# Sixty-two throwaway 64-column products more on TensorE in a network of fp32 matmuls

## The chip, the cores and the metric

The kernel runs on one core of one Trainium2 chip. The metric is the device time of one execution in microseconds (us). The median of three runs of the kernel before is 2643.28 us, from 2640.35 to 2643.76.

## What is computed

A chain of 16 blocks is applied to 256 tokens of width 1024, all in fp32. First come four pairs of a mixer and an MLP. The mixers are a gated delta rule (twice, `gdn`), an mLSTM (`mlstm`) and a differential attention (`diff`). The MLP is `square(relu(h @ w1)) @ w2` with a hidden width of 4096. Then come two layers of four blocks each: a SwiGLU block of width 2816 (`ffn1`), a hybrid mixer of a gated scan and a forgetting attention (`hybrid`), a cross attention on 256 memory tokens (`cross`) and a second SwiGLU block (`ffn2`). Every block ends by adding to the stream:

```python
def sq_relu_mlp(h, w1, w2):
    return jnp.square(jax.nn.relu(h @ w1)) @ w2
...
def swiglu(h, w_gate, w_up, w_down):
    return (jax.nn.silu(h @ w_gate) * (h @ w_up)) @ w_down
...
        h = rms_norm(x, norm_g[i, 2])
        x = x + rms_norm(sq_relu_mlp(h, mlp_w1[i], mlp_w2[i]), norm_g[i, 3])
```

## The kernel before, in words

**Precision.** A product of two fp32 matrices is made of three products of rounded parts. ScalarE rounds a slab of weights to `wH` (line 1517), and VectorE takes the remainder `wL` (line 2167). The activations are split in the same way into `hH` and `hL`, or into areas of the tile `hidden_parts`. TensorE then sums `wH*hH`, `wH*hL` and `wL*hH` into one PSUM region. The helper `three` (line 630) issues this for one 128 x 256 output: eight chunks of the contraction times three pairs, so 24 products. Each product loads a 128 x 128 stationary operand and streams 256 columns. All TensorE products go through the helper `mm`, so the trace shows nearly all of them under line 621, and they are told apart by their tiles.

**Weights.** They come in slabs of 1 MB. A slab of an input projection is 256 output channels wide, so two calls of `three` use it, 48 products. `to_channels` (line 696) makes channels by tokens, with the weights as the stationary operand. `to_tokens` (line 711) makes tokens by channels, with the activations stationary, one call of `three` for each tile of 128 tokens. It is used for the "value" slabs: four in `mlstm`, four in `diff` (there each of the eight tiles is called by itself, between two heads of the attention, by `values`, line 1324), two in each `hybrid`, and four in the second `cross`.

**The order of a part.** A part is one block. `first_products` (line 653) opens each of the 16 parts. It interleaves the products of the part's first two slabs, 96 in all, so that they can follow the activations chunk by chunk: it waits for `low_split` of the first slab (line 660), then for `hH_ready` before each pair of chunks (line 670), later for `hL_ready`. Ahead of it TensorE makes the sum of squares of the norm, and while the norm is finished on the other engines it has other work or nothing. Behind eight of the parts this is `fill` (line 731), 48 products of a memory projection that a later block needs, issued in pieces; elsewhere it is `keep_running` (line 727), plain products of ones.

**The delta rule.** In `gdn` the 16 slabs of the projection are the loop at line 1070. From its fifth slab on it waits until the bank written four slabs ago has been read (`evac`, line 1079). Other steps stand between slabs: score products behind slab 7, and transposes `turn_values` of four blocks behind slabs 11 to 14. Slab 15 stands apart, behind `leaf_level`.

**The throwaway product.** `settle` (line 723) issues one product of 64 columns into a region that the next product overwrites, so its result is used by nothing. It stands in front of the second half of slabs 2 and 9 of `mlp_w1`, in front of the second half of steps 2 and 12 of the SwiGLU projections, and before the fifth slab of each down projection (lines 704, 895, 904, 920, 929), 24 times in all:

```python
            def settle(last, bank, c0):
                mm(ps[:, bank, c0:c0 + 64], hL[:, 1, 0:P], hH[:, 0, 0:64], True, True)
```

Of the kernel before, what the change touches and what calls it, by code (L numbers as in the profile page):

```python
# [15 lines left out]
P = 128  # L16
T = 256
# [146 lines left out]
def program(nc, io, out, parts=None):  # L164
# [30 lines left out]
    with ExitStack() as ctx:  # L195
# [5 lines left out]
        def sem(name):  # L201

            if not name.startswith(SHARED):
                name = scope[0] + name
            if name not in sems:
                sems[name] = ctx.enter_context(nc.semaphore(name))
            return sems[name]
# [39 lines left out]
        onesR = sb("onesR", [P, T], F32R)  # L247
# [368 lines left out]
        def _(pe):  # L616
# [13 lines left out]
            def three(dst, w, x, chunks, before=None, first=True, last=True, second="x"):  # L630


                ins = None
                for pair in (((0, 0), (0, 1), (1, 0)) if second == "x" else ((0, 0), (1, 0), (0, 1))):
                    for k in range(chunks):
                        if before:
                            before(pair, k)
                        ins = mm(dst, w[pair[0]](k), x[pair[1]](k), first and pair == (0, 0) and k == 0,
                                 last and pair == ((1, 0) if second == "x" else (0, 1)) and k == chunks - 1,
                                 **({"skip_group_check": True} if chunks == 1 else {}))  # L640
                return ins
# [11 lines left out]
            def first_products(name, layer, js, c, at, src=(hH, hL), together=True):  # L653


                n = [slab_no[(name, layer, j)] for j in js]
                xH, xL = src
                high_w = [high(n[0], c)] + ([high(n[1], c)] if together else [])
                low_w = [low(n[0], c), low(n[1], c)]
                pe.wait_ge(sem("low_split"), n[0] + 1)  # L660

                def both_halves(b, w, x, k, start=False, ends=False):
                    for m in range(2):
                        ins = mm(ps[:, 4 + b, m * T:(m + 1) * T], at(w, k, m), x[:, k, :],
                                 start and k == 0 and m == 0, ends and k == DC - 1 and m == 1,
                                 skip_group_check=True)
                    return ins

                for k0 in range(0, DC, 2):
                    pe.wait_ge(sem("hH_ready"), W.next("hH_ready"))  # L670
                    for k in (k0, k0 + 1):
                        both_halves(0, high_w[0], xH, k, start=True)
                    for k in (k0, k0 + 1):
                        both_halves(0, low_w[0], xH, k)
                    for k in (k0, k0 + 1) if together else ():
                        both_halves(1, high_w[1], xH, k, start=True)
                if not together:
                    high_w.append(high(n[1], c))
                    for k in range(DC):
                        both_halves(1, high_w[1], xH, k, start=True)  # L680
                for k in range(DC):
                    if k % 2 == 0:
                        pe.wait_ge(sem("hL_ready"), W.next("hL_ready"))
                    last = both_halves(0, high_w[0], xL, k, ends=True)
                last.then_inc(sem("products_done"), 1)
                for k in range(DC):
                    both_halves(1, high_w[1], xL, k)
                pe.wait_ge(sem("low_split"), n[1] + 1)
                for k in range(DC):
                    last = both_halves(1, low_w[1], xH, k, ends=True)  # L690
                last.then_inc(sem("products_done"), 1)
# [4 lines left out]
            def to_channels(name, layer, j, bank, src=(hH, hL), free=None, settled=False):  # L696

                n = slab_no[(name, layer, j)]
                wh, wl = high(n, DC), low(n, DC)
                if free and j >= 4:  # L700
                    pe.wait_ge(sem(free), W.next(free))
                for m in range(2):
                    if settled and m == 1:
                        settle(last, bank, T)
                    last = three(ps[:, bank, m * T:(m + 1) * T],
                                 [lambda k: wh[:, k, m * P:(m + 1) * P], lambda k: wl[:, k, m * P:(m + 1) * P]],
                                 [lambda k: src[0][:, k, :], lambda k: src[1][:, k, :]], DC,
                                 low_weights(n, (1, 0)) if m == 0 else None)
                last.then_inc(sem("products_done"), 1)

            def to_tokens(name, layer, j, bank, src=(hH, hL), tiles=range(TT)):

                n = slab_no[(name, layer, j)]
                wh, wl = high(n, DC), low(n, DC)
                for i in tiles:
                    last = three(ps[:, bank, i * T:(i + 1) * T],
                                 [lambda k: src[0][:, k, i * P:(i + 1) * P], lambda k: src[1][:, k, i * P:(i + 1) * P]],
                                 [lambda k: wh[:, k, :], lambda k: wl[:, k, :]], DC,
                                 low_weights(n, (0, 1)) if i == 0 else None, second="w")
                if TT - 1 in tiles:  # L720
                    last.then_inc(sem("products_done"), 1)

            def settle(last, bank, c0):

                mm(ps[:, bank, c0:c0 + 64], hL[:, 1, 0:P], hH[:, 0, 0:64], True, True)

# [162 lines left out]
            def mlp(i):  # L889
                first_products("mlp_w1", i, (0, 1), DC, columns)  # L890
                summed_norm()
                for j in range(2, 16):
                    if j == 2:
                        filler_out(filled_before[("mlp", i)])
                    to_channels("mlp_w1", i, j, bank_of(j), free="bank_read", settled=j in (2, 9))
                    if i == 0 and j == 3:
                        summed_norm(3, "xsq_summed")

                def floor():
                    pe.wait_ge(sem("bank_read"), W.next("bank_read", 4))  # L900
                    norm_floor()

                down_product("mlp_w2", i, 32, range(0, 32, 2), floor, end_by_pairs=True,
                             at_fifth=lambda last: settle(last, 4, 0))
                post_sum(pair_first=True, on_floor=True, filler=fills[("mlp", i)], upto=34 if i == 2 else 48)

            def ffn(kind, l):
                first_products(kind, l, (0, 1), 2 * DC, lambda w, k, half: w[:, half * DC + k, :], src=ffn_x,
                               together=(kind, l) == ("ffn1", 0))
                summed_norm()  # L910
                for n in range(2, 22):
                    u = slab_no[(kind, l, n)]
                    wh, wl = high(u, 2 * DC), low(u, 2 * DC)
                    if n == 2:
                        filler_out(filled_before[(kind, l)])
                    if n >= 4:
                        pe.wait_ge(sem("bank_read"), W.next("bank_read"))
                    for half in range(2):
                        if n in (2, 12) and half == 1:
                            settle(last, 4 + n % 4, T)  # L920
                        last = three(ps[:, 4 + n % 4, half * T:(half + 1) * T],
                                     [lambda k: wh[:, half * DC + k, :], lambda k: wl[:, half * DC + k, :]],
                                     [lambda k: ffn_x[0][:, k, :], lambda k: ffn_x[1][:, k, :]], DC,
                                     low_weights(u, (1, 0)) if half == 0 else None)
                    last.then_inc(sem("products_done"), 1)

                def settled(last):
                    pe.wait_ge(sem("bank_read"), W.next("bank_read", 4))
                    settle(last, 4, 0)

                down_product(f"{kind}_w_down_2", l, 22, range(22), at_fifth=settled)

# [15 lines left out]
            def gdn(i):  # L948
# [121 lines left out]
                for p in range(2, 16):  # L1070
# [6 lines left out]
                        break  # L1077
                    if p >= 4:
                        pe.wait_ge(sem("evac"), evacuated(p - 4))
                    to_channels("gdn_w_in", j, GDN_ORDER[p], 4 + p % 4)  # L1080
                    if j == 0 and p == 2:
                        pe.wait_ge(sem("vector_setup"), VECTOR_SETUP["params_ready"])
# [1811 lines left out]
```

## Time and profile before

| | us |
|---|---|
| median of three runs | 2643.28 |
| lowest and highest run | 2640.35, 2643.76 |
| profiled execution, its own time | 2639.53 |
| its span, first to last instruction | 2637.8 |
| TensorE busy in it | 2578.1 (98%) |
| VectorE busy | 1668.8 (63%) |
| ScalarE busy | 1357.2 (51%) |
| granted TensorE clock, mean | 0.997 |

The profile holds one execution. Around its span of 2637.8 us lie 1.7 us that the time of 2639.53 also counts. TensorE's matmuls are pipelined, and the end of each is modelled: a row of 8 products that spans 1.07 us does not mean that the next row begins 1.07 us later. The distance from the start of one row to the start of the next is the time that the row's products took, and all working with paces below uses starts.

### The profile page before, as it was taken

To read this page: it belongs to the slowest core of one execution; us is meant where nothing else is said; L and a number is where in the kernel's file an instruction comes from. 1 tells how busy PE (TensorE), PEld (TensorE's weight loads), DVE (VectorE), ACT (ScalarE), POOL (GpSimd) and SP (SyncE) were. 2 spreads that over 40 slices of the span, in tenths; PEclk is the share of its full clock that TensorE was granted. 3 is DMA by queue.
4 is the path that set the end of the run, shared out by engine and by line. 5 is a ranking of instruction groups with operands and counts; after the bars stand their busy time and mean duration, and the time that the engine had idled before them with its cause. 6 is when DMAs were issued, how large, how long until landed. Compare 5 with 4: busy or idle time off the path is not lost.

```text
span 2637.8 us, 48807 instructions
## 1 busy us (share of the span) xinstructions
PE 2578.1 (98%) x21538; PEld 2516.6 (95%) x21538; DVE 1668.8 (63%) x1988; ACT 1357.2 (51%) x1687; POOL 163.0 (6%) x259
## 2 busy tenths in 40 slices
PE   8999999999999999999999999999999999999998
PEld 8989999899998999999999999999999999999998
DVE  5667556575586655676646656756656657764764
ACT  5745445554456544665535445555445436544543
POOL 4400000000020000420000000000000000000000
PEclk9999999999999999999999999999999999999999
DMA  7515565456554664533666765444766755344763
GB/s 215 170 33 160 193 239 164 144 180 224 181 168 148 193 240 148 155 122 118 206 240 171 195 225 169 135 154 136 198 195 185 196 194 161 113 136 138 195 196 128
DMA packets 430995, 452.43 MB, mean 172 GB/s; under 512 B 14114, under 2 KB 395792, under 8 KB 428608
## 3 DMA queue, kind: packets, MB, share of 16 engines
q1 hardware_dynamic: 417952, 416.05, 50.6%
q0 software_dynamic: 8336, 32.87, 3.6%
q8 instruction: 170, 2.79, 0.4%
q10 hardware_dynamic: 4496, 0.39, 0.1%
q14 instruction: 41, 0.34, 0.0%
HBM read 441.15 MB, written 7.60 MB: 170 GB/s over the span
## 4 chain that ended last, share of the span: by engine, by line
PE 85%; DVE 6%; ACT 6%; DMA 1%; issue 1%; POOL 1%; ACTq 0%; SPq 0%; DVEq 0%
PE ps L621 84%; ACT wH L1517 2%; DVE wL L2167 2%; ACT hidden_parts L1577 1%; DMA ring<-in_gdn_w_in 0%; DVE arena L2742 0%; ACT L1544 0%; POOL arena L508 0%; PE ps L1052 0%; DVE hT L2423 0%; POOL arena L510 0%; PE ps L1270 0%; DVE sq L2250 0%; DVE arena L2431 0%; DMA arena<-leaf_out 0%
## 5 line engine op out<-in xcount | busy, mean ns | idle before, releaser
L2167 DVE TENSOR_TENSOR wL<-ring,wH 128x2048 fp32r<-128x2048 f32 x392 | 898.6, 2293 | 744.6 <-ACT wH L1517 744.2
L1517 ACT ACTIVATE wH<-ring 128x2048 fp32r<-128x2048 f32 x392 | 753.6, 1922 | 988.8 <-PE ps L621 986.6
L621 PE MATMUL ps<-hidden_parts,wH 128*128 128x256 f32 x6656 | 989.5, 277 | 3.8 <-ACT hidden_parts L1577 2.8
L621 PEld LDWEIGHTS ps<-hidden_parts,wH 128*128 128x128 f32 x6656 | 899.6, 188 | 5.9 <-issue 3.6
L621 PE MATMUL ps<-hidden_parts,wL 128*128 128x256 f32 x3328 | 693.2, 276 | 1.5 <-DVE wL L2167 1.5
L621 PEld LDWEIGHTS ps<-hidden_parts,wL 128*128 128x128 f32 x3328 | 521.9, 188 | 1.8 <-DVE wL L2167 1.8
L621 PE MATMUL ps<-hH,wH 128*128 128x256 f32 x2624 | 366.1, 281 | 6.4 <-DVE hH L2184 3.1
L621 PE MATMUL ps<-hH,wL 128*128 128x256 f32 x2624 | 358.9, 278 | 3.5 <-DVE wL L2167 3.5
L621 PE MATMUL ps<-hL,wH 128*128 128x256 f32 x2624 | 347.7, 279 | 0.0
L621 PEld LDWEIGHTS ps<-hH,wH 128*128 128x128 f32 x2624 | 329.1, 189 | 12.6 <-issue 10.5
L621 PEld LDWEIGHTS ps<-hH,wL 128*128 128x128 f32 x2624 | 326.9, 188 | 4.3 <-DVE wL L2167 4.3
L621 PEld LDWEIGHTS ps<-hL,wH 128*128 128x128 f32 x2624 | 323.2, 189 | 0.0
L621 PE MATMUL ps<-arena 128*128 128x128 f32 (+1 forms) x1392 | 227.3, 309 | 16.2 <-ACT arena L1941 7.2
L621 PEld LDWEIGHTS ps<-arena 128*128 128x128 f32 x1392 | 193.9, 192 | 34.7 <-ACT arena L1941 9.6
L621 PE MATMUL ps<-sq,onesR 128*128 128x256 f32 (+1 forms) x184 | 64.2, 483 | 4.5 <-ACT sq L1599 2.8
L2423 DVE SCALAR_TENSOR_TENSOR hT<-hT,arena 128x255 f32<-128x255 f32 (+1 forms) x144 | 61.7, 497 | 7.5 <-ACT hT L1751 7.2
L2323 DVE TENSOR_TENSOR arena<-ps,rs 128x512 f32<-128x512 f32 x88 | 60.3, 685 | 0.1
L621 PEld LDWEIGHTS ps<-sq,onesR 128*128 128x128 f32 x184 | 33.5, 197 | 19.8 <-issue 7.3
L621 PE MATMUL ps<-hidden_parts 128*128 128x256 f32 x384 | 51.3, 288 | 0.0
L621 PEld LDWEIGHTS ps<-hidden_parts 128*128 128x128 f32 x384 | 48.1, 191 | 0.6
L2278 DVE TENSOR_TENSOR arena<-arena,ps 128x512 f32<-128x512 f32 x64 | 43.6, 681 | 5.6 <-ACT arena L1669 5.6
L1686 ACT ACTIVATE hidden_parts<-arena 128x512 fp32r<-128x512 f32 x64 | 40.2, 629 | 11.6 <-DVE arena L2278 11.6
(324 smaller groups left out, 1971.7 us busy)
## 6 DMA issues: line engine op xcount, KB each, us to landing
ring<-in_mlp_w SPq DMA_DIRECT2D x128, 1024.0 KB, 5.4
ring<-in_ffn_w_gate SPq DMA_DIRECT2D x88, 512.0 KB, 4.0
ring<-in_ffn_w_up SPq DMA_DIRECT2D x88, 512.0 KB, 5.3
ring<-in_ffn_w_down SPq DMA_DIRECT2D x44, 1024.0 KB, 5.0
ring<-in_gdn_w_in SPq DMA_DIRECT2D x32, 1024.0 KB, 5.9
ring<-in_w_in SPq DMA_DIRECT2D x28, 1024.0 KB, 5.4
hidden_parts<-mem_parts POOLq DMA_DIRECT2D x14, 1024.0 KB, 6.9
ring<-in_mlstm_w_in SPq DMA_DIRECT2D x12, 1024.0 KB, 5.3
```

The lines of the kernel that those rows point to most:

```text
L621: return pe.matmul(o, l, r, start=start, stop=stop, **k)
L1517: f(wH[:, n % PARTS, :], ring[:, n % RING, :], ACT.Copy).then_inc(sem("high_split"), 1)
L1577: ins = f(x_parts[0][:, k, :], xT[:, k, :], ACT.Copy, scale=column(gain, k0 + k))
L1686: f(hidH[:, 2 * g:2 * g + 2, :], two(prod_s[:, g % 2, :]), ACT.Copy).then_inc(sem("hiddenH_ready"), 1)
L2167: tt(wL[:, n % PARTS, :], ring[:, n % RING, :], wH[:, n % PARTS, :].bitcast(F32), ALU.subtract)\
L2278: tt(prod_s[:, g % 2, :], act_s[:, g % 2, :], ps[:, 4 + g % 4, :], ALU.mult)\
L2323: tt(two(act_s[:, n % 2, :]), two(ps[:, 4 + n % 4, :]), rs_twice(), ALU.mult)\
L2423: ins = stt(dst, src, w, dst, ALU.mult, ALU.add)
```

## The change

One throwaway product of 64 columns is added in three kinds of places:

- in `first_products`, behind the wait for the first slab's low part and ahead of the wait for the first activations, into bank 4 from `onesR`: once in each of the 16 parts
- in `to_tokens`, in front of each tile of 128 tokens: 8 times each in `mlstm`, `diff` and the second `cross`, 4 times in each `hybrid`, 32 in all
- in the loop of `gdn`, in front of slabs 8 to 14: 7 times in each of the two, 14 in all

The argument `last` of `settle`, which it did not use, goes. The 24 old ones stay.

```diff
@@ first_products
                 pe.wait_ge(sem("low_split"), n[0] + 1)
+                mm(ps[:, 4, 0:64], onesR[:, 0:P], onesR[:, 0:64], True, True)
...
@@ to_tokens
                 for i in tiles:
+                    settle(bank, i * T)
                     last = three(ps[:, bank, i * T:(i + 1) * T],
...
-            def settle(last, bank, c0):
+            def settle(bank, c0):
...
@@ gdn
                     if p >= 4:
                         pe.wait_ge(sem("evac"), evacuated(p - 4))
+                    if p >= 8:
+                        settle(4 + p % 4, 0)
                     to_channels("gdn_w_in", j, GDN_ORDER[p], 4 + p % 4)
```

The order of TensorE's instructions differs by these additions alone. At the start of the `mlstm` part, behind the 42 fill products (`hidden_parts`), the difference reads:

```order
 L621 MATMUL ps<-sq,onesR 128x256 x3
 L621 MATMUL ps<-hidden_parts 128x256 x42
+L621 MATMUL ps<-onesR 128x64
 L621 MATMUL ps<-hH,wH 128x256 x4
 L621 MATMUL ps<-hH,wL 128x256 x4
```

The new product (+) stands between the fill and the first product of the slab. In the same part, at the value slabs, whose rows have `wH` or `wL` as the moving operand:

```order
 L621 MATMUL ps<-hH,hidden_parts 40x256 x8
+L621 MATMUL ps<-hH,hL 128x64
 L621 MATMUL ps<-wH,hH 128x256 x8
 L621 MATMUL ps<-wH,hL 128x256 x8
 L621 MATMUL ps<-wL,hH 128x256 x8
+L621 MATMUL ps<-hH,hL 128x64
 L621 MATMUL ps<-wH,hH 128x256 x8
```

There one stands in front of every 24 products.

## Rows read from the trace of the kernel before

**Rows 1.** Page: busy time by engine, granted clock, chain that ended last
```profile
PE 2578.1 (98%) x21538; PEld 2516.6 (95%) x21538; DVE 1668.8 (63%) x1988; ACT 1357.2 (51%) x1687; POOL 163.0 (6%) x259
...
PEclk9999999999999999999999999999999999999999
...
PE 85%; DVE 6%; ACT 6%; DMA 1%; issue 1%; POOL 1%; ACTq 0%; SPq 0%; DVEq 0%
```

**Rows 2.** Groups by form: the throwaway products that stand there already
```profile
L621 PE MATMUL ps<-hH,hL 128*128 128x64 f32 x24 | 4.7, 194 | 0.0
```

**Rows 3.** Timeline, PE, 546 to 552: start us, us, engine, line, operation, tiles, count
```profile
546.89 1.10 PE L621 MATMUL ps<-hL,wH 128*128 128x256 f32 x8
547.83 1.12 PE L621 MATMUL ps<-hH,wL 128*128 128x256 f32 x8
548.79 0.20 PE L621 MATMUL ps<-hH,hL 128*128 128x64 f32 x1
548.83 1.17 PE L621 MATMUL ps<-hH,wH 128*128 128x256 f32 x8
549.84 1.07 PE L621 MATMUL ps<-hL,wH 128*128 128x256 f32 x8
550.74 1.07 PE L621 MATMUL ps<-hH,wL 128*128 128x256 f32 x8
```

**Rows 4.** Timeline, PE, 269.9 to 275, another of the 24
```profile
270.84 1.07 PE L621 MATMUL ps<-hH,wL 128*128 128x256 f32 x8
271.75 0.19 PE L621 MATMUL ps<-hH,hL 128*128 128x64 f32 x1
271.78 1.18 PE L621 MATMUL ps<-hH,wH 128*128 128x256 f32 x8
272.80 1.07 PE L621 MATMUL ps<-hL,wH 128*128 128x256 f32 x8
273.70 1.07 PE L621 MATMUL ps<-hH,wL 128*128 128x256 f32 x8
```

**Rows 5.** Timeline, PE, 533 to 538: first products of the second MLP
```profile
532.73 1.84 PE L621 MATMUL ps<-hidden_parts 128*128 128x256 f32 x14
534.40 0.63 PE L621 MATMUL ps<-hH,wH 128*128 128x256 f32 x4
534.88 0.63 PE L621 MATMUL ps<-hH,wL 128*128 128x256 f32 x4
535.35 1.11 PE L621 MATMUL ps<-hH,wH 128*128 128x256 f32 x8
```

**Rows 6.** Timeline, PE: first products behind idle time, two parts, [idle <-releaser]
```profile
217.54 0.71 PE L621 MATMUL ps<-hH,wH 128*128 128x256 f32 x4 [1.33 <-ACT hH L1577]
...
1820.87 0.71 PE L621 MATMUL ps<-hidden_parts,wH 128*128 128x256 f32 x4 [0.59 <-ACT hidden_parts L1577]
```

**Rows 7.** Timeline, PE, value slabs of mlstm: first tile and last tile
```profile
430.00 1.07 PE L621 MATMUL ps<-wH,hH 128*128 128x256 f32 x8
...
449.04 1.07 PE L621 MATMUL ps<-wH,hH 128*128 128x256 f32 x8
```

**Rows 8.** Timeline, PE, value slabs of the second cross: first, second, last tile
```profile
2383.66 2.05 PE L621 MATMUL ps<-wH,hidden_parts 128*128 128x256 f32 x16
...
2386.49 2.05 PE L621 MATMUL ps<-wH,hidden_parts 128*128 128x256 f32 x16
...
2403.45 2.05 PE L621 MATMUL ps<-wH,hidden_parts 128*128 128x256 f32 x16
```

**Rows 9.** Timeline, PE, 766 to 772: first value tile of diff
```profile
768.76 1.10 PE L621 MATMUL ps<-wH,hL 128*128 128x256 f32 x8
769.71 1.10 PE L621 MATMUL ps<-wL,hH 128*128 128x256 f32 x8
```

**Rows 10.** Timeline, PE, second gdn: starts of slabs 9 and 10, inside slab 12
```profile
1112.64 1.11 PE L621 MATMUL ps<-hH,wH 128*128 128x256 f32 x8
...
1118.29 1.11 PE L621 MATMUL ps<-hH,wH 128*128 128x256 f32 x8
...
1130.96 1.07 PE L621 MATMUL ps<-hL,wH 128*128 128x256 f32 x8
1131.87 1.07 PE L621 MATMUL ps<-hH,wL 128*128 128x256 f32 x8
```

**Rows 11.** Timeline, PE, 727 to 730: four narrow products between wide ones
```profile
728.52 0.51 PE L621 MATMUL ps<-onesR,hidden_parts 128*128 128x2 f32 x4
728.89 1.16 PE L621 MATMUL ps<-hH,wH 128*128 128x256 f32 x8
```

More of the change, by code:

```diff
@@ L703, in to_channels @@
                     if settled and m == 1:
-                        settle(last, bank, T)
+                        settle(bank, T)
                     last = three(ps[:, bank, m * T:(m + 1) * T],
@@ L903, in mlp @@
                 down_product("mlp_w2", i, 32, range(0, 32, 2), floor, end_by_pairs=True,
-                             at_fifth=lambda last: settle(last, 4, 0))
+                             at_fifth=lambda last: settle(4, 0))
                 post_sum(pair_first=True, on_floor=True, filler=fills[("mlp", i)], upto=34 if i == 2 else 48)
@@ L919, in ffn @@
                         if n in (2, 12) and half == 1:
-                            settle(last, 4 + n % 4, T)
+                            settle(4 + n % 4, T)
                         last = three(ps[:, 4 + n % 4, half * T:(half + 1) * T],
@@ L928, in settled @@
                     pe.wait_ge(sem("bank_read"), W.next("bank_read", 4))
-                    settle(last, 4, 0)
+                    settle(4, 0)
                 down_product(f"{kind}_w_down_2", l, 22, range(22), at_fifth=settled)
```

## The prediction

> **What bounds the kernel now.** I read the page first: TensorE is busy 98% of the span, its granted clock is at the upper of its two levels, 2.4 GHz, in every slice, and the chain that ended last lies on it for 85% [rows 1]. So nearly every nanosecond of TensorE's own order is a nanosecond of the kernel, and the question is what its products cost each. The groups by form do not tell this, since the ends of products are modelled; I therefore went to the timeline of TensorE and took distances between the starts of rows. What is to be seen there is that the same product, 256 columns with a new stationary operand, runs at two paces. In [rows 7] the value slabs of mlstm take 449.04 - 430.00 = 19.04 us for seven tiles of 24, so 113.3 ns each. In [rows 8] those of cross take 2403.45 - 2383.66 = 19.79 us for as many, 117.8 ns each. I call these the fast and the slow pace. They differ by 4.5 ns, or 4%. No wait is recorded in either stretch, and engines and clock are the same. Once at a pace the stream keeps it until something other than such a product comes between.
>
> The third thing to see is what the 24 throwaway products do that are already there [rows 2]. In [rows 3] one stands behind a slow stretch: the row ahead of it takes 547.83 - 546.89 = 0.94 us for eight products, and the row two behind it 550.74 - 549.84 = 0.90. The stream was slow and is fast. In [rows 4] one stands in a fast stretch: 0.90 or 0.91 before, 0.90 behind. I looked at all 24: 6 of them stand behind a slow stretch and 18 behind a fast one, and behind each of the 24 the pace is fast. That is good evidence that the product does what its name says, where it has wide products before and behind it.
>
> **What one costs.** In [rows 4], from the throwaway product to the second row behind it is 272.80 - 271.75 = 1.05 us, for one throwaway and eight products; eight products alone take 0.91. So one costs 0.14 us, paid in full because the engine has no idle time there. [Rows 3] give the same 1.05 us. The start of the next product lies only 0.03 to 0.04 us behind it, but the product after that comes late, so the 0.03 is not its price. The Trainium skill ("TensorE: Matmul & The Clock Gate", Back-to-back issue gap) gives N/2.4 + 2.5 ns from one isolated warm matmul to the next, 29 ns at 64 columns, and says itself that this leaves out the weight load. At that price my sum below would come out near -5.6 us in place of +0.4; the trace disagrees, with 0.14 us. For a place with narrow products around it the trace has one bound from below: four products of 2 columns take 728.89 - 728.52 = 0.37 us, so 0.09 each [rows 11]. I take 0.14 everywhere, since most places lie between wide products, and keep 0.09 for the range.
>
> One pays for itself if it turns slow into fast for more than 0.14 us / 4.5 ns = 31 products. With this the three kinds of places come apart.
>
> **The first products, 16.** I looked up the stretch in front of each. In eight parts TensorE goes without idle time from fill or from plain products into the slab, and in all eight the first products are slow; [rows 5] are one of them: the rows of the slab follow at 0.47 to 0.48 us for four. There the slow pace lasts for the 96 products of `first_products` in mlstm, diff and both hybrids, where other kinds of products follow, and for 120 in three MLPs and in the first ffn1, until the old throwaway product in slab 2. Saved: 4 x 96 + 4 x 120 = 864 products x 4.5 ns = 3.9 us. Paid: 8 x 0.14 = 1.1. In the other eight parts TensorE is idle for 0.4 to 1.8 us until the first activations have been rounded [rows 6]. The new product waits only for the weights, so it runs in that idle time and costs nothing; for the same reason the stream starts from rest behind it as before, and I count no gain. Of these eight starts four are fast and four slow now, the slow ones for some 30 products each (0.14 us each). This term: 1.1 - 3.9 = -2.8 us.
>
> **The value slabs, 32.** Here one stands in front of every 24 products, less than the 31 that pay for it. In mlstm and the hybrids the stretch is fast already [rows 7]: 16 are paid and nothing is saved. In cross all 192 products are slow [rows 8]: 192 x 4.5 = 0.86 us. In diff each tile stands alone between heads of the attention, and seven of the eight are slow; [rows 9] show one, with 0.95 us for eight. They save 168 x 4.5 = 0.76 us. No idle time of TensorE lies within these stretches that could cover the cost. Paid: 32 x 0.14 = 4.5. This term: 4.5 - 0.86 - 0.76 = +2.9 us.
>
> **The delta-rule slabs, 14.** [Rows 10] show a slow slab, 5.65 us for 48 products, and the inside of a fast one, 0.91 for eight. By the timeline eight of the 14 are slow (slabs 11 and 14 of the first gdn; 8, 9, 10, 11, 13 and 14 of the second) and six fast. Saved: 8 x 48 x 4.5 = 1.7 us. Paid: 14 x 0.14 = 2.0. Slab 15 stands behind other work and keeps its own pace. This term: +0.3 us. Many of these slabs have transposes in front, where no old throwaway product stands, so here it is open whether it works as well.
>
> **The sum.** -2.8 + 2.9 + 0.3 = +0.4 us. Against the profiled execution's own 2639.53 us that gives 2639.9. This execution lies 3.8 us under the median of the runs shown, so against the median it is 2643.7. The 54 products that are paid for cost 7.6 us and win back 7.2: a change that does something at 24 or so places and in which the parts cancel. The weights are not late anywhere for it: ScalarE's rounding waits for TensorE, which frees the slabs, and both other engines are under two thirds busy [rows 1]. Nothing is queued behind a new wait, as there is none.
>
> **Rivals.**
>
> *The throwaway product is cheap.* If its price were the 0.03 us between its start and the next one [rows 3], 54 would cost 1.6 us and the sum would be 1.6 - 7.2 = -5.6 us: 2637.7. The Trainium skill (same page and section) would give 0.03 us as well, by the formula above. For it speaks only that the start of the next product follows so closely; against it stand both readings of 1.05 us. Chance 0.06, with whatever else might make it much faster, such as slow stretches elsewhere falling away as well (all wide products at the slow pace in the span together would be worth about 16 us).
>
> *The pace does not turn where it matters.* The 24 old ones stand within streams of wide products of one kind. The new ones in diff and gdn stand behind narrow products or transposes, those of `first_products` behind fill and with another stationary tile, and a semaphore wait comes between them and the stream. If a stream that begins behind such a change takes its pace anew, all 54 are paid and nothing is saved: +7.6 us, 2650.9, slower by 0.29%. It decides from the point where less than a third of the 7.2 us comes back. For it speaks that streams behind other products and behind idle time start at either pace [rows 6, 10]; against it the 24 of 24. Chance 0.08.
>
> *Luck at the starts.* Each start from rest may fall the other way once times shift by fractions of a microsecond. Eight starts at 0.14 to 0.5 us make about 1 us either way. This is no case by itself but a part of the range.
>
> **How the numbers follow.** A measurement of this kernel tells about 0.2%, 5.3 us, from no change. The forecast, with chance 0.86, lies within that: from 0.09 us as the price of the 22 in narrow surroundings (-1.1), the slow starts from rest turning fast (-0.6) and the runs' own spread below the median (-2.9), which gives 2639.1, up to half of the saving failing (+3.6) and the spread above it (+0.5), which gives 2647.8. I take 2639 to 2648. Faster 0.06, within 0.2% 0.86, slower 0.08.
>
> **What would show it.** In the profile of the changed kernel there must be 24 + 32 + 14 = 70 products of 64 columns with `hL` and 16 with `onesR`. Right: the rows behind fill in the eight parts come at 0.45 us for four and 0.91 for eight; the tile of mlstm's values takes 2.72 + 0.14 = 2.86 us, that of cross goes from 2.83 to the same 2.86; a gdn slab comes at about 5.6 whether it was slow or fast. Wrong: rows at 0.94 behind a new throwaway product (the second rival), or a mlstm tile at 2.75 (the first). The forecast as a whole would be wrong if paces changed in stretches that the change does not touch, above all in the 1,400 products in a row of an MLP, where one change of pace that lasted would be worth up to 6 us.

## The result and the profile after

The kernel got slower. Over 12 runs of each, the median went from 2643.94 us (2637.32 to 2648.22) to 2649.90 us (2647.41 to 2654.55); the ratio is 1.0024, with a 95% interval of 1.0016 to 1.0033. That is +6 us where +0.4 was forecast, above the stated range of 2639 to 2648. The profiled execution took 2647.41 us, with a span of 2645.6 against 2637.8. The clock does not explain the rise: the granted clock averages 0.9952 over the 12 executions of the changed kernel, and 0.9949 to 0.9955 over the executions of before that stand beside the experiments below.

The page of the changed kernel shows what the page of before showed [rows 1], the chain on TensorE for 85% as before, with 62 products more:

```profile
PE 2584.4 (98%) x21600; PEld 2523.9 (95%) x21600; DVE 1669.1 (63%) x1988; ACT 1357.4 (51%) x1687; POOL 161.1 (6%) x259
```

The groups by form of the changed kernel have all 86 products of 64 columns, 70 of the old kind and 16 of ones (compare [rows 2]):

```profile
L621 PE MATMUL ps<-hH,hL 128*128 128x64 f32 x70 | 14.7, 210 | 0.0
...
L621 PE MATMUL ps<-onesR 128*128 128x64 f32 x16 | 3.6, 226 | 2.6 <-DVE wL L2171 2.6
```

So the added products stand where they were meant to. What they do to the pace is in the timeline. First the value slabs of mlstm, which ran at 0.91 us for eight in [rows 7] (start us, us, engine, line, operation, tiles, count):

```profile
433.40 0.19 PE L621 MATMUL ps<-hH,hL 128*128 128x64 f32 x1
...
434.42 1.07 PE L621 MATMUL ps<-wH,hL 128*128 128x256 f32 x8
435.33 1.07 PE L621 MATMUL ps<-wL,hH 128*128 128x256 f32 x8
436.23 0.19 PE L621 MATMUL ps<-hH,hL 128*128 128x64 f32 x1
...
437.29 1.10 PE L621 MATMUL ps<-wH,hL 128*128 128x256 f32 x8
438.23 1.10 PE L621 MATMUL ps<-wL,hH 128*128 128x256 f32 x8
439.18 0.19 PE L621 MATMUL ps<-hH,hL 128*128 128x64 f32 x1
```

The first tile is fast, 435.33 - 434.42 = 0.91 us for eight. The throwaway product at 436.23 has a fast stretch ahead of it and a slow one behind it: 438.23 - 437.29 = 0.94. From throwaway to throwaway the second tile takes 2.95 us, where a tile took 2.72 before. The other six of mlstm's eight tiles read the same, and so do all eight of the two hybrids, which were fast before. In cross, whose tiles were slow before [rows 8], they stay slow, also where the stream ahead is fast, as it is ahead of the first tile:

```profile
2388.91 0.20 PE L621 MATMUL ps<-hH,hL 128*128 128x64 f32 x1
...
2390.91 1.10 PE L621 MATMUL ps<-wL,hidden_parts 128*128 128x256 f32 x8
2391.85 0.19 PE L621 MATMUL ps<-hH,hL 128*128 128x64 f32 x1
```

That is 2391.85 - 2388.91 = 2.94 us a tile where it was 2.83. The first products of mlstm, behind fill, as one of the seven parts of this kind; they answer to [rows 5]:

```profile
404.80 1.72 PE L621 MATMUL ps<-hidden_parts 128*128 128x256 f32 x13
406.36 0.19 PE L621 MATMUL ps<-onesR 128*128 128x64 f32 x1
...
406.94 0.64 PE L621 MATMUL ps<-hH,wL 128*128 128x256 f32 x4
407.41 0.87 PE L621 MATMUL ps<-hH,wH 128*128 128x256 f32 x6
```

The fill itself comes at (406.36 - 404.80) / 13 = 120 ns, and the rows behind it still at 407.41 - 406.94 = 0.47 us for four, the slow pace, in all seven. Last the delta-rule slabs of the second gdn, slow in [rows 10]:

```profile
1111.73 0.28 PE L621 MATMUL ps<-hH,hL 128*128 128x64 f32 x1
...
1112.85 1.07 PE L621 MATMUL ps<-hL,wH 128*128 128x256 f32 x8
1113.76 1.07 PE L621 MATMUL ps<-hH,wL 128*128 128x256 f32 x8
```

Here it works: 0.91 us for eight, and so in 13 of the 14 slabs.

One thing lies beside the change. In this execution part of 24 products of the second cross ran at the lower clock level, behind an idle time of 2.57 us that before has, too (2.56 us). From 2408 to 2424 us the granted clock is 0.89, and 1.00 in the same stretch of before, 2402 to 2418. The 24 products span 7.13 us where they span 5.45 before: 1.7 us of this profile's 7.8. In the profiles of the value tiles alone and of the changed kernel's second set they span 5.45 us again, so it is no part of the cause.

### The profile page after: what moved, and what is told of

Its sections match the earlier page's. It is cut to its first block, busy times and chain, and to the rows that moved or that the text cites. A ratio compares the mean times of both kernels' runs of the same rounds, so it can differ in the third digit from the quotient of the medians.

```text
span 2645.6 us, 48909 instructions
## 1 busy us (share of the span) xinstructions
PE 2584.4 (98%) x21600; PEld 2523.9 (95%) x21600; DVE 1669.1 (63%) x1988; ACT 1357.4 (51%) x1687; POOL 161.1 (6%) x259
## 4 chain that ended last, share of the span: by engine, by line
PE 85%; DVE 6%; ACT 6%; DMA 1%; issue 1%; POOL 1%; ACTq 0%; SPq 0%; DVEq 0%; POOLq 0%
PE ps L621 84%; ACT wH L1521 2%; DVE wL L2171 2%; ACT hidden_parts L1581 1%; DMA ring<-in_gdn_w_in 0%; POOL arena L510 0%; DVE arena L2746 0%; ACT L1548 0%; PE ps L1054 0%; DVE hT L2427 0%; POOL arena L508 0%; PE ps L1274 0%; DVE sq L2254 0%; DVE arena L2435 0%; ACT sq L1790 0%
```

## The experiments

The question was why a product that had turned the pace to fast in 24 of 24 places did not do so in the new ones, and what each of the three groups is worth. The first four runs take the groups apart.

**The first products alone.**

```diff
 in to_tokens and in gdn, against the changed kernel:
-                    settle(bank, i * T)
-                    if p >= 8:
-                        settle(4 + p % 4, 0)
```

> Only the 16 throwaway products of the first products are kept. Theory A (what follows decides the pace; one made of ones behind fill does not turn it): 8 are paid at 0.11 to 0.14 us, nothing is saved, some idle starts move; +1 to +2 us. Rival B (it turns the pace, and the profile of the changed kernel was an odd execution): -2.8 us. In the trace, A has the first products behind fill at 0.94 us for eight, B at 0.91.

Measured: 2645.50 us against 2644.87, ratio 1.0000 (0.9991 to 1.0008). The seven parts behind fill are slow again. The saving of 3.9 us does not exist. The price of the eight that are paid, 1.1 us by the prediction, is too small to be told from nothing here. The expected +1 to +2 us lie inside the interval, at its upper end (+2.1). The eighth part without idle time, the second hybrid, stands behind plain products of ones and not behind fill; it is slow here and fast in the changed kernel.

**The value tiles alone.**

```diff
 against the kernel before, in to_tokens:
+                    settle(bank, i * T)
```

> Only the 32 throwaway products in front of the value tiles are kept. Theory A: each costs 0.11 us or more and leaves the tile slow, 2.94 us from tile to tile where it was 2.72; mlstm and the two hybrids lose 0.2 us a tile, cross 0.1; together +4 to +6 us, less what the slabs behind them gain if those turn fast. Rival B (each costs 0.14 us and the tile is fast, 2.86): +2.9 us.

Measured: 2648.68 us, ratio 1.0017 (1.0009 to 1.0026), so +3.8 us between the medians. Theory A had +4 to +6 less what the slabs behind gain. The timeline has the same pattern as the changed kernel, tile for tile: the throwaway products ahead of mlstm's first three tiles start at 433.31, 436.14 and 439.09, so the first tile takes 2.83 us and the second 2.95.

**The delta-rule slabs alone.**

```diff
 against the kernel before, in gdn:
+                    if p >= 8:
+                        settle(4 + p % 4, 0)
```

> Only the 14 throwaway products of the delta-rule slabs are kept. Theory A (in front of channel slabs it turns the pace, as the 24 old ones do): 0 to +0.5 us, with all slabs but perhaps one at 0.91 us for eight. Rival B (the pace is luck of each execution): some 7 of the 14 slow, +1 us.

Measured: 2643.43 us against 2644.87, ratio 0.9996 (0.9988 to 1.0005). All 14 slabs are fast. One of them, and the end of the slab ahead of it:

```profile
1117.80 1.07 PE L621 MATMUL ps<-hH,wL 128*128 128x256 f32 x8
1118.71 0.19 PE L621 MATMUL ps<-hH,hL 128*128 128x64 f32 x1
...
1124.29 0.19 PE L621 MATMUL ps<-hH,hL 128*128 128x64 f32 x1
```

From 1118.71 to 1124.29 is 5.58 us for 48 products and one throwaway, 0.14 more than 48 x 113.3 ns. In front of channel slabs the sum of the prediction is right in its parts.

**No throwaway product at all**, the old 24 included.

```diff
             def settle(bank, c0):
-                mm(ps[:, bank, c0:c0 + 64], hL[:, 1, 0:P], hH[:, 0, 0:64], True, True)
+                return
```

> The kernel before without any throwaway product: its old 24 are taken out too. Theory A (they turn 6 slow stretches fast and cost 0.11 to 0.14 us each): 3 us are saved, and the 6 stretches that were slow ahead of one stay slow for up to 340 more products at 4.5 ns each, 6 to 9 us, so the time rises by 3 to 6 us. Rival C (a slow stretch ends by itself within some products): 3 us faster.

Measured: 2659.67 us against 2644.87, ratio 1.0063 (1.0051 to 1.0075), so +15 us. I had +3 to +6: a slow pace that nothing breaks can last far longer than the 340 products that I gave it. In the first ffn1 the timeline reads, at its third slab,

```profile
1437.67 1.11 PE L621 MATMUL ps<-hidden_parts,wL 128*128 128x256 f32 x8
1438.61 1.58 PE L621 MATMUL ps<-hidden_parts,wH 128*128 128x256 f32 x12
```

0.94 us for eight products, and still 0.36 for three at its end, 170 us later (0.34 at the fast pace):

```profile
1605.73 0.40 PE L621 MATMUL ps<-hidden_parts,wH 128*128 128x256 f32 x2
...
1606.09 0.40 PE L621 MATMUL ps<-hidden_parts,wH 128*128 128x256 f32 x2
```

In the 181 us from 1424 on there are 1,539 products, all at the slow pace, with a granted clock of 1.00. This slow stretch does not end by itself, and rival C falls for it. But in three of the MLPs the slow stretch behind fill does end, without any throwaway product, at one product that comes late. The second MLP shows it:

```profile
549.18 1.10 PE L621 MATMUL ps<-hL,wH 128*128 128x256 f32 x8
550.12 1.11 PE L621 MATMUL ps<-hH,wL 128*128 128x256 f32 x8
551.06 1.07 PE L621 MATMUL ps<-hH,wH 128*128 128x256 f32 x8
551.97 1.07 PE L621 MATMUL ps<-hL,wH 128*128 128x256 f32 x8
```

The row at 549.18 takes 0.94 us and the one at 551.06 takes 0.91. Between them stands one product whose successor starts 144 ns later and not 118; it is the first that uses `wL` of its slab, which VectorE had finished at 549.99. The other two turn in the same way, at 870.04 and 1255.52. It also goes the other way. In the kernel before, the product at 1552.49 is followed after 149 ns and not 113, and the fast stream is slow from there to the old throwaway product at 1563.60; the same stands at 1952.79. Over all profiles, most products that come late by as much leave the pace as it was. So a throwaway product is not the only thing at which a stream takes its pace anew: a delay of 30 ns can be enough. The old 24 pay because the slow pace can last, and from one of them to the next, or to the end of its stream, there are some 340 to 650 products.

The next four ask what decides. They change the operands, the place or the width.

**Own operands in front of the value tiles.**

```diff
 against the run with the value tiles alone:
-                    settle(bank, i * T)
+                    mm(ps[:, bank, i * T:i * T + 64], src[0][:, 0, i * P:(i + 1) * P], wh[:, 0, 0:64], True, True)
```

> As the run with the 32 value-tile products alone, but the throwaway product takes its operands from the product behind it: activations stationary, weights moving. Theory A1 (the kind of operands must be that of the stream that follows): tiles turn fast, 2.86 us from tile to tile, and the time falls from +3.8 us to +2 or +3. Theory A2 (in front of a stream with weights moving no throwaway product gives the fast pace): tiles stay at 2.94 and the time at +3.8 us.

Measured: 2652.55 us against 2643.36, ratio 1.0027 (1.0019 to 1.0036). All 32 tiles are slow, the first of mlstm too. The channel slabs behind the value slabs now stay slow as well; they were fast with the old operands. That is 288 products at 4.5 ns, 1.3 us of the difference to the run before; the rest of it is not clear of the noise. Behind mlstm's values with own operands, and with the old ones in the changed kernel:

```profile
456.26 1.10 PE L621 MATMUL ps<-hH,wH 128*128 128x256 f32 x8
457.20 1.11 PE L621 MATMUL ps<-hL,wH 128*128 128x256 f32 x8
```

```profile
457.73 1.07 PE L621 MATMUL ps<-hL,wH 128*128 128x256 f32 x8
458.64 1.07 PE L621 MATMUL ps<-hH,wL 128*128 128x256 f32 x8
```

0.94 against 0.91 for eight. Theory A1 falls.

**Own operands ahead of the first products.**

```diff
 against the kernel before, in first_products:
                     pe.wait_ge(sem("hH_ready"), W.next("hH_ready"))
+                    if k0 == 0:
+                        mm(ps[:, 4, 0:64], at(high_w[0], 0, 0), xH[:, 0, 0:64], True, True)
```

> One 64-column product in each of the 16 first products, behind the wait for the first activations, made of the first slab's weights and these activations. Theory A1 (operands decide): the eight parts behind fill turn fast, 0.91 us for eight, 3.9 us saved, 16 x 0.12 = 1.9 us paid: -2 us. Theory A2 (the stream ahead, the fill at 120 ns, decides): they stay slow, +1.9 us.

Measured: 2643.34 us against 2643.36, ratio 1.0003 (0.9993 to 1.0014). Behind fill all seven stay slow, A1 falls here as well:

```profile
404.00 0.74 PE L621 MATMUL ps<-hH,wH 128*128 128x64 f32 x5
...
405.05 1.11 PE L621 MATMUL ps<-hH,wH 128*128 128x256 f32 x8
406.00 0.64 PE L621 MATMUL ps<-hH,wL 128*128 128x256 f32 x4
```

(The row's form is that of its first product, so x5 is the throwaway one and four others.) 406.00 - 405.05 = 0.95 us for eight.

**Twice the width.**

```diff
 against the run with the value tiles alone:
+                    mm(ps[:, bank, i * T:i * T + 128], hL[:, 1, 0:P], hH[:, 0, 0:128], True, True)
```

> As the run with the 32 value-tile products alone, with 128 columns in place of 64. If the pace behind it hangs on how far the next weight load is shifted (theory A3), the tiles may turn fast: 2.86 to 2.89 us from tile to tile; if on the kind of stream, they stay slow at 2.94 or more.

One execution, 2652.34 us. All of mlstm's tiles are slow, with the same cost as at 64 columns, although the next product starts 0.07 us behind it and not 0.03:

```profile
436.85 0.23 PE L621 MATMUL ps<-hH,hL 128*128 128x128 f32 x1
...
437.91 1.10 PE L621 MATMUL ps<-wH,hL 128*128 128x256 f32 x8
438.85 1.10 PE L621 MATMUL ps<-wL,hH 128*128 128x256 f32 x8
439.79 0.22 PE L621 MATMUL ps<-hH,hL 128*128 128x128 f32 x1
```

2.94 us a tile. So the width does not decide the pace here, and it is not the price either: 0.11 us at 64 and at 128 columns, about what a product of 256 columns takes. All of them load one stationary operand, so the load is the likely price; no run changes the load alone. (In diff two of the eight tiles were fast, as in the changed kernel.)

**Ones behind the wait.**

```diff
 against the kernel before, in first_products, behind the wait for hH_ready:
+                    if k0 == 0:
+                        mm(ps[:, 4, 0:64], onesR[:, 0:P], onesR[:, 0:64], True, True)
```

> The 16 products of ones stand behind the wait for the first activations instead of ahead of it, alone. Operands as in the change, place as in the run with own operands: tells place from operands. Theory A1: still slow behind fill, 0.94 us for eight; if the place decides, fast, 0.91. The starts behind idle time are paid now, 0.1 us each.

One execution, 2640.85 us. Behind fill the rows are those of the changed kernel, 0.94 us for eight:

```profile
407.88 1.11 PE L621 MATMUL ps<-hH,wH 128*128 128x256 f32 x8
408.82 0.40 PE L621 MATMUL ps<-hH,wL 128*128 128x256 f32 x2
```

So at that spot neither the operands nor the side of the wait matter. What is left is what stands directly ahead, the fill, whose products come at 120 ns. The next run keeps the operands and moves the product a few places on.

**Eight products inside the first products.**

```diff
 against the kernel before, in first_products, behind the eight products of the first two chunks:
+                    if together and k0 == 0:
+                        mm(ps[:, 5, 0:64], at(high_w[0], 0, 0), xH[:, 0, 0:64], True, True)
                     for k in (k0, k0 + 1) if together else ():
```

> The kernel before with 10 throwaway products more, made of the slab's weights and activations, each inside the first products, 8 products behind their start (in the 10 parts that do both slabs together; 8 of them come without idle time and are slow). Theory A4 (behind the fill nothing turns the pace, but within a stream of products with weights stationary one does): these 8 turn fast from there on, 88 to 112 products each, 3.5 us saved, 1.4 paid: -2 us. Theory A5 (the interleaved first products themselves do not hold the fast pace): they stay at 0.94 us for eight, +1.4 us.

Measured: 2642.51 us against 2644.51, ratio 0.9991 (0.9981 to 1.0001). All eight parts that were slow turn fast (A4):

```profile
406.03 1.20 PE L621 MATMUL ps<-hH,wH 128*128 128x64 f32 x9
407.07 0.62 PE L621 MATMUL ps<-hH,wL 128*128 128x256 f32 x4
407.52 1.07 PE L621 MATMUL ps<-hH,wH 128*128 128x256 f32 x8
408.43 0.62 PE L621 MATMUL ps<-hH,wL 128*128 128x256 f32 x4
```

408.43 - 407.52 = 0.91 us for eight. The size fits the expected -2 us, though the interval reaches 1. The second gdn turns fast as well. In the first MLP, where the stream came from rest and was fast already, the same product turned it slow.

**All the places that pay**: this, nine of the 14 delta-rule ones, and one in front of slab 8 of mlstm.

```diff
+                    if p in (8, 12, 13, 14) or (p == 11 and j == 0):
+                        settle(4 + p % 4, 0)
...
+                    if s == 8:
+                        settle(bank_of(s), 0)
```

> As that, and 9 of the 14 delta-rule ones (those behind other work: slabs 8, 12, 13, 14 of both, 11 of the first), one in front of slab 8 of the mlstm projection (193 products that were slow behind the value slabs), none in front of value tiles. If the rule of the runs so far holds (in front of channel slabs it turns the pace): all these stretches fast; saved 3.5 + 1.7 + 0.8, paid 20 x 0.12 = 2.4: -3 to -4 us, about 0.13% faster.

Measured: 2643.30 us against 2644.51, ratio 0.9992 (0.9981 to 1.0002). In its profile, with a span of 2634.8 us, all places are fast but two, the first MLP's again and that of the second gdn's first products. Both streams came from rest and were fast ahead of it. In the first MLP:

```profile
218.38 0.62 PE L621 MATMUL ps<-hH,wL 128*128 128x256 f32 x4
218.83 1.22 PE L621 MATMUL ps<-hH,wH 128*128 128x64 f32 x9
219.88 0.63 PE L621 MATMUL ps<-hH,wL 128*128 128x256 f32 x4
220.35 0.91 PE L621 MATMUL ps<-hH,wH 128*128 128x256 f32 x6
```

0.45 us for four ahead of it, 220.35 - 219.88 = 0.47 behind.

**Without those two parts.**

```diff
-                    if together and k0 == 0:
+                    if together and k0 == 0 and (name, layer) not in (("mlp_w1", 0), ("gdn_w_in", 1)):
```

> 18 throwaway products more than before: 8 inside the first products that come without idle time, 9 in front of delta-rule slabs that follow other work, one in front of slab 8 of the mlstm projection. All stretches behind them fast; saved about 6 us, paid 18 x 0.12 = 2.2: -3 to -4 us by the sum, 0.1 to 0.15%, near the limit of what is measurable.

Measured: 2640.18 us against 2642.07, ratio 0.9995 (0.9986 to 1.0004). All 18 places are fast. The saving is smaller than the 3 to 4 us of the sum. Each of the three versions lies just below before, and each interval reaches 1: a gain of 1 or 2 us is likely and not shown.

**Inside the value tiles.**

```diff
 against the kernel before, in to_tokens, for mlstm, ahead of the ninth product of a tile:
+                            mm(ps[:, 3, 0:64], src[0][:, 0, i * P:(i + 1) * P], wh[:, 0, 0:64], True, True)
```

> The kernel before with 8 throwaway products in the value tiles of mlstm alone, each 8 products behind the start of its tile, into a bank that is not in use. If the kind of stream decides (weights moving), the pace behind them is slow, 0.94 us for eight, as in the change; if the place at the start of the tile decides, it is fast, 0.91.

One execution, 2642.45 us. The pace behind it is slow in all eight tiles, from a fast stream in the first:

```profile
434.19 1.10 PE L621 MATMUL ps<-wL,hH 128*128 128x256 f32 x8
435.13 1.13 PE L621 MATMUL ps<-wH,hH 128*128 128x256 f32 x9
```

434.19 to 435.13 is 0.94 (the x9 holds the next throwaway product). So it is the kind of stream, weights moving and activations stationary, and not the place at its start. Whether it matters which operand is stationary, or where the operands lie, no run separates.

**The changed kernel once more.**

> The changed kernel once more, unaltered. Theory A (what stands ahead and behind decides): the 16 value tiles of mlstm and the hybrids, 15 of them slow in the first profile, are slow again, the 7 first products behind fill too, the delta-rule slabs but one fast; time +0.2 to +0.3%. Rival B (luck of one execution): the pattern differs at half of the places.

Measured: 2650.20 us against 2641.20, ratio 1.0034 (1.0019 to 1.0048). The pattern repeats: 16 of 16 tiles of mlstm and the hybrids slow (15 before), 8 of 8 of cross, the same two tiles of diff fast, seven of seven behind fill slow, this time 14 of 14 delta-rule slabs fast. Several of the eight starts from rest fell otherwise. Rival B falls, except for these starts.

## Why the prediction was wrong

**What bounds the kernel, and the two paces.** Right: TensorE's order is the time, and 113.3 and 117.8 ns a product are in every profile. Not right is that a stream keeps its pace until something other than such a product comes between. One late product was enough in three MLPs of the run without throwaway products (0.94 us for eight ahead, 0.91 behind), and at 1552.49 and 1952.79 of before.

**"Behind each of the 24 the pace is fast."** True, and the step from it is the one that failed. The prediction said of the new places that it was "good evidence that the product does what its name says, where it has wide products before and behind it", and then counted it for value tiles and first products. It also holds in all 14 profiles that have them. But all 24 stand in front of a stream with weights stationary and none directly behind fill. I had read 24 cases of one kind as a rule for all. The runs put in its place: in front of channel slabs it gives the fast pace (all 24, and 41 of 42 delta-rule places in three runs); in front of a value tile of mlstm, the hybrids or cross it gives or keeps the slow pace (118 of 120 places in five runs; the exception is the first tile of mlstm, twice, behind products with a stationary operand of 40 columns), and inside one too (8 of 8); directly behind fill it changes nothing (7 of 7 in each of five runs). Eight products into the first products it left the fast pace at 25 of 28 places in three runs; at the other three it turned a fast stream slow.

**The first products, forecast -2.8 us.** Measured 0 (-2.4 to +2.1). The saved 3.9 us were not there. That it runs for nothing where TensorE idles was right: its wait in the groups is for `wL`, and the starts come when the activations do.

**The value slabs, forecast +2.9 us.** Measured +3.8 between medians, ratio 1.0017. The term looks near, but by two errors against each other. Of the 16 tiles that were fast, 15 lose 0.22 us each where 0.14 was paid, 3.3 us in all; cross loses 0.11 a tile where 0.03 was forecast, 0.9 us; and diff has two fast tiles where it had one, not eight, so it pays about 0.8 us net. Against that, the channel slabs behind the value slabs of mlstm and the hybrids, which the prediction left out, turn from slow to fast. Before, slab 8 of mlstm begins with

```profile
451.76 1.11 PE L621 MATMUL ps<-hH,wH 128*128 128x256 f32 x8
452.70 1.10 PE L621 MATMUL ps<-hL,wH 128*128 128x256 f32 x8
```

at 0.94 us for eight; after, it is at 0.91 (above, beside the run with own operands), for 192 products 0.9 us. In the hybrids it is one slab each, 96 products, 0.4 us. That adds up to 3.3 + 0.1 (the sixteenth tile) + 0.9 + 0.8 - 0.9 - 0.4 = +3.8 us, as measured.

**The delta-rule slabs, forecast +0.3 us.** Measured -1.1 us by the ratio (-3.2 to +1.3): right within what can be told.

**The price.** 0.14 us in a fast stretch was right in front of channel slabs. The one value tile that stays fast pays less: 436.23 - 433.40 = 2.83 us, 0.11 over 2.72. In a slow stretch it is 2.94 - 2.83 = 0.11. The rival that it costs 0.03 is refuted by every tile.

**The sum.** The three groups alone give ratios of 1.0000, 1.0017 and 0.9996, together 1.0013; the whole gives 1.0024 and 1.0034 in two sets. The intervals allow both, but nearly half of the 6 us is not assigned to a group by the runs. In the profile of the changed kernel slow stretches also stand in the first MLP, which the change does not touch beyond its start. The same window, after and then before:

```profile
240.00:270.00 30.00, 29.75 (x254) 29.56 (x253) 21.89 (x22) 16.13 (x18) 0.00 (x0) 1.00 0.63 205
```

```profile
240.00:270.00 30.00, 29.75 (x262) 29.56 (x262) 22.03 (x21) 16.84 (x19) 0.00 (x0) 1.00 0.64 200
```

254 products in 30 us, then 262. The slow stretch begins at a short wait for `wL`, and before has the same wait, with a fast stream behind it. After, then before:

```profile
244.26 1.21 PE L621 MATMUL ps<-hH,wL 128*128 128x256 f32 x8 [0.25 <-DVE wL L2171]
```

```profile
243.51 1.20 PE L621 MATMUL ps<-hH,wL 128*128 128x256 f32 x8 [0.25 <-DVE wL L2167]
```

A second one begins in the same way at 365.50, behind 1.28 us of idle time for `wL` that before has at 363.68. Together they make this MLP 2.3 us longer: from the norm's first product ahead of it to the next norm's it is 400.01 - 212.38 = 187.6 us, and 396.94 - 211.63 = 185.3 before. Such stretches differ between the profiles of all versions; whether the change makes them more frequent stays open. Counted over whole traces, the changed kernel has as many slow products as before: 3,548 and 3,560 products in its two profiles are followed after 115.5 to 121.5 ns, and 3,493 in the one of before (the profiles of its three parts alone have 3,392, 3,458 and 3,794, so one profile tells this to some 200 products, 1 us). What is fast in some places is slow in others. What is left is the price, by an estimate 54 products at 0.11 to 0.14 us, so 5.9 to 7.6 us, and 6 were measured.

**The rivals.** "The pace does not turn where it matters", with 2650.9 us and a chance of 0.08, was the case, and named one place rightly ("those of `first_products` behind fill and with another stationary tile"). But it sought the others in diff and gdn, not in the value slabs of mlstm, and assumed that nothing is won at 54 places; in truth the slow delta-rule slabs won and 15 tiles lost a second time. A hint was in the trace of before: the channel slabs directly behind the fast value slabs of mlstm and both hybrids were slow, so a change of the stream's kind moved the pace. Cross [rows 8] is no such hint, since the stream was slow there already ahead of the values.

## What to carry to other kernels

When a trick is known to work from places of one kind, check what the kind is (which operand is stationary, what stands ahead, how long the stream is) before it is copied to places of another. Here a throwaway product cost 0.11 to 0.14 us at 64 and at 128 columns, about as much as a full one, so at 4% a stream needs some 30 products behind it to pay, and in front of a short or already fast stream it can only lose. Take paces from the starts of neighbouring rows of the timeline, since busy times and mean durations hide a loss of 4%.

## What the runs showed of the hardware

The same product runs at 113.3 or 117.8 ns. A stream can keep the slow pace for long: 1,539 products in 181 us in the run without throwaway products, at a granted clock of 1.00. The stream takes its pace anew at a product of few columns, and it can do so behind a short wait (0.25 us at 244.26 in the changed kernel) or a single late product (144 ns in place of 118 at 550.12, without throwaway products). What comes out behind a product of 64 columns depends on the stream. It is mostly fast with weights stationary: at the old 24 places in all 14 profiles that have them and at 41 of 42 delta-rule places, but three places in the first products turned from fast to slow. It is mostly slow with weights moving: 118 of 120 places in mlstm, the hybrids and cross, while in diff two of the eight tiles were fast in four profiles of five. It is unchanged directly behind products at 120 ns, but fast eight products later. 128 columns in place of 64 give the same time, 2.94 us a tile. Without the old 24 the kernel takes 15 us more, 0.6%. What in the machine makes the two paces stays open; no run here shows it.
